# A hybrid decoder step on one core: GpSimd's weight split for the mixers in half-size instructions

## The chip, the cores and the metric
One Trainium2 chip, one of its cores. The metric is device time in microseconds (us) from the start to the end of one execution; lower is better. Five engines of the core work side by side, each through its own queue of instructions in order, and wait for each other on semaphores: TensorE (matmuls; PE in the profile, its weight loads PEld), VectorE (DVE), ScalarE (ACT), GpSimd (POOL) and SyncE (SP, which issues DMAs here).

## What is computed
Two layers of a hybrid decoder over 512 prompt tokens and 32 sample tokens (8 sequences of 4), all float32. Cut to what matters here:

```python
xn = _rmsnorm(h, g_mix)
proj = jnp.einsum('bld,de->ble', xn, w_in)             # inputs of three mixers
o_a = gla(...)        # gated linear attention, 4 heads, chunks of 64
o_m = mlstm(...)      # matrix memory, 4 heads
o_d = diff_attention(...)   # differential attention, paged cache for the samples
gates = jax.nn.sigmoid(jnp.einsum('bld,de->ble', xn, w_gate)).reshape(B, L, 3, D)
merged = (gates[:, :, 0] * jnp.einsum('blv,vd->bld', o_a, w_a)
          + gates[:, :, 1] * jnp.einsum('blv,vd->bld', o_m, w_m)
          + gates[:, :, 2] * jnp.einsum('blv,vd->bld', o_d, w_d))
h = h + jnp.einsum('bld,de->ble', merged, w_out)
h = h + (silu(rms(h) @ w_ffn_gate) * (rms(h) @ w_ffn_up)) @ w_ffn_down
h = h + sigmoid(rms(h) @ w_ple_gate) * (p_l @ w_ple_proj)
```

## The kernel before
Activations lie transposed: 128 channels on the partitions, 544 tokens (512 + 32) along a row. Each weight matrix is cut into chunks of up to 8 blocks of 128 x 128 (`raw`, 1024 columns, 512 KB). Each chunk is split in two for the matmuls: `wH`, the weight rounded to the matmul's format (fp32r), and `wL`, the rest (`raw` minus `wH`). TensorE multiplies wH by xH, wH by xL and wL by xH for each block, in two halves of 272 tokens, so that a chunk is 48 matmuls (line 536, `blocks_product`). Four buffers hold `raw`, two hold `wH` and two `wL`: the split of chunk n waits until TensorE has done chunk n - 2 (`chunk_done`), and TensorE's chunk n waits for `wl_split`. SyncE's load of chunk n waits for the `wl_split` of chunk n - 4.

Outside the mixers ScalarE makes `wH` (lines 465, 520 and 1851) and GpSimd `wL` (lines 469 and 528). In the mixers ScalarE has other work, and GpSimd makes both (`both_loop`, lines 481 and 484): 60 chunks a layer, named ml, df, merge0, merge1 and merge2, 12 each. Between its `wH` and its `wL` GpSimd waits for its own signal `wh_split`.

In that stretch TensorE's order is written out by hand: the small matmuls of the three mixers, and between them pieces of the next chunks' products, a quarter of a chunk each (`fill`). A piece that opens a new output waits for `out_taken`, which VectorE signals as it takes the output two before from PSUM (lines 688, 1744, 1754 and 1758, with the sequencer's signals at 1746 and 1755). VectorE does these takings in its own queue, behind its part of the mixers: the cumulated gates of gla (lines 954 to 965), the rotation of q and k (1212 to 1218), the keys and scores of the mLSTM (1239 to 1271), the softmax weights of the attention (`maxima` 1540; `weights` 1547 to 1550), the scaling and splitting of a branch's output (674 and 680; the latter signals `bn_l`, for which the last branch products wait), the sample's softmax (1580 to 1582) and the sum of the merged branches (1760). After the pieces between the attention's steps, what is left of merge2 is multiplied chunk by chunk without a break (`fill.rest`).

Of the kernel before, what the change touches and what calls it, by code (L numbers as in the profile page):

```python
# [28 lines left out]
F32 = mybir.dt.float32  # L29
F32R = mybir.dt.float32r  # L30
I32 = mybir.dt.int32
ALU = mybir.AluOpType
# [3 lines left out]
P = 128  # L36
D = 1024
KD = D // P
# [19 lines left out]
RAW, SPLIT = 4, 2  # L58
# [36 lines left out]
def program(nc, a, c, o):  # L95
    ctx = ExitStack()
    with ctx:
# [37 lines left out]
        ones = fixed.put("ones", [P, P])  # L135
# [35 lines left out]
        raw = [ws.put(f"raw{i}", [P, KMAX, P]) for i in range(RAW)]  # L171
        wH = [ws.put(f"wH{i}", [P, KMAX, P], F32R) for i in range(SPLIT)]
        wL = [ws.put(f"wL{i}", [P, KMAX, P], F32R) for i in range(SPLIT)]
# [122 lines left out]
        s, sems = Semaphores(), []  # L296
# [175 lines left out]
        def both_loop(pool, name, count=12, per=4):  # L472

            base = CHUNK[name]
            with pool.Fori(0, count // per) as i:
                for j in range(per):
                    n = base + j
                    pool.wait_ge(s.w_in[n % RAW], w_count(n, i, per))
                    pool.wait_ge(s.chunk_done, n + per * i - (SPLIT - 1))

                    pool.tensor_tensor(wH[n % SPLIT][:, :, :], raw[n % RAW][:, :, :],  # L481
                                       ones[:, 0:1].unsqueeze(1).to_broadcast([P, KD, P]), ALU.mult).then_inc(s.wh_split, 1)
                    pool.wait_ge(s.wh_split, n + 1 + per * i)
                    pool.tensor_tensor(wL[n % SPLIT][:, :, :], raw[n % RAW][:, :, :], wH[n % SPLIT][:, :, :].bitcast(F32),  # L484
                                       ALU.subtract).then_inc(s.wl_split, 1)

        def w_count(slot_chunk, i, per):

            slot = slot_chunk % RAW
            more = 48 if slot == CHUNK["small"] % RAW and slot_chunk >= CHUNK["small"] else 0  # L490
            return 16 * (slot_chunk // RAW + 1) + more + 16 * (per // RAW) * i
# [216 lines left out]
        with nc.Fori(0, DEPTH) as layer:  # L708
# [4 lines left out]
            with nc.Block() as block:  # L713
# [154 lines left out]
                @block.gpsimd  # L868
                def _(pool):
                    for n in range(SPLIT):  # L870
                        low_chunk(pool, n)
                    for k in range(1, KD):
                        add_square(pool, 0, k, sq0)
                    for n in range(SPLIT, 4):
                        low_chunk(pool, n)
                    low_loop(pool, "gla", 12, lambda j: KD, first=1)
                    low_loop(pool, "small", 1, lambda j: KD, per=1)
                    for name in ("ml", "df", "merge0", "merge1", "merge2"):
                        both_loop(pool, name)
                    low_loop(pool, "out", 8, lambda j: KD)  # L880
                    low_loop(pool, "ffn", 2 * KF, lambda j: KD)
                    low_loop(pool, "down", 4 * KD, lambda j: DOWN_K[j % 4][1], per=8)
                    for n in range(10):
                        low_chunk(pool, CHUNK["ple"] + n)
# [1342 lines left out]
```

## Time and profile before
| | |
|---|---|
| median of 3 runs | 2559.25 us (2553.18 to 2563.7) |
| the profiled execution | 2556.49 us |
| its span, first to last instruction | 2554.7 us |
| TensorE busy | 2359.1 us (92%) |
| VectorE busy | 1067.4 us (42%) |
| GpSimd busy | 1051.9 us (41%) |
| ScalarE busy | 690.3 us (27%) |

An engine's busy time is the union of its instructions; waits of its sequencer are not in it. The two layers run the same program (the mixers of layer 0 lie at about 116 to 755 us, those of layer 1 at 1370 to 2008). In the lists, "A <- B: us, times, longest" means that engine A stood idle until B released it. A row of the timeline gives the start, the duration, the engine, the line, the operation, what it writes and reads, and in brackets the idle time before it. A duration on VectorE or GpSimd counts from the instruction's start, also where it then waits for something inside it.

### The profile page before, as it was taken

To read this page: it belongs to the slowest core of one execution; us is meant where nothing else is said; L and a number is where in the kernel's file an instruction comes from. 1 tells how busy PE (TensorE), PEld (TensorE's weight loads), DVE (VectorE), ACT (ScalarE), POOL (GpSimd) and SP (SyncE) were. 2 spreads that over 40 slices of the span, in tenths; PEclk is the share of its full clock that TensorE was granted. 3 is DMA by queue.
4 is the path that set the end of the run, shared out by engine and by line. 5 is a ranking of instruction groups with operands and counts; after the bars stand their busy time and mean duration, and the time that the engine had idled before them with its cause. 6 is when DMAs were issued, how large, how long until landed. Compare 5 with 4: busy or idle time off the path is not lost. (4 is left out here: it accounts for less than half of the span.)

```text
span 2554.7 us, 43509 instructions
## 1 busy us (share of the span) xinstructions
PE 2359.1 (92%) x17974; PEld 2263.6 (89%) x17974; DVE 1067.4 (42%) x1289; ACT 690.3 (27%) x1006; POOL 1051.9 (41%) x472
## 2 busy tenths in 40 slices
PE   4989898989999999999969998978999999999996
PEld 3978797878899999999968988977898999999995
DVE  3173653641335443312534537356224444342236
ACT  3130313322214222222232131233222332222222
POOL 3444344432454444344344443434336444444431
PEclk9999899998999999999989999989899999999998
DMA  3522315223332332223135141331332323232221
GB/s 99 143 58 61 75 50 107 63 76 91 92 116 85 91 88 84 77 87 100 34 95 130 51 97 40 53 113 55 100 113 70 114 87 90 83 88 77 89 85 43
DMA packets 370870, 213.87 MB, mean 84 GB/s; under 512 B 34290, under 2 KB 356950, under 8 KB 370210
## 3 DMA queue, kind: packets, MB, share of 16 engines
q1 hardware_dynamic: 369186, 205.11, 29.3%
q10 hardware_dynamic: 1536, 6.69, 0.7%
q8 instruction: 106, 1.74, 0.3%
q14 instruction: 42, 0.34, 0.1%
HBM read 195.88 MB, written 15.88 MB: 83 GB/s over the span
## 5 line engine op out<-in xcount | busy, mean ns | idle before, releaser
L536 PE MATMUL G<-xH,wH 128*128 128x272 f32 x3616 | 789.6, 300 | 76.0 <-DVE xL L596 43.0
L536 PE MATMUL G<-xH,wL 128*128 128x272 f32 x3616 | 761.9, 293 | 0.0
L536 PE MATMUL G<-xL,wH 128*128 128x272 f32 x3616 | 760.9, 293 | 0.0
L536 PEld LDWEIGHTS G<-xH,wH 128*128 128x128 f32 x3616 | 581.2, 193 | 106.7 <-issue 54.2
L528 POOL TENSOR_TENSOR wL<-raw,wH 128x1024 fp32r<-128x1024 f32 (+2 forms) x186 | 421.3, 2265 | 599.1 <-ACT wH L1851 290.4
L536 PEld LDWEIGHTS G<-xL,wH 128*128 128x128 f32 x3616 | 583.3, 193 | 0.0
L536 PEld LDWEIGHTS G<-xH,wL 128*128 128x128 f32 x3616 | 579.4, 194 | 0.0
L481 POOL TENSOR_TENSOR wH<-raw,ones 128x1024 fp32r<-128x1024 f32 x120 | 234.3, 1953 | 698.0 <-PE G L536 691.9
L484 POOL TENSOR_TENSOR wL<-raw,wH 128x1024 fp32r<-128x1024 f32 x120 | 301.7, 2514 | 9.4
L465 ACT ACTIVATE wH<-raw 128x1024 fp32r<-128x1024 f32 (+2 forms) x116 | 105.5, 911 | 375.6 <-PE G L536 344.4
L1851 ACT ACTIVATE wH<-raw 128x1024 fp32r<-128x1024 f32 x82 | 87.0, 1061 | 325.8 <-PE G L536 325.8
L536 PE MATMUL G<-hidH,wL 128*128 128x272 f32 x704 | 145.7, 288 | 0.0
L536 PE MATMUL G<-hidH,wH 128*128 128x272 f32 x704 | 145.5, 288 | 0.0
L536 PE MATMUL G<-hidL,wH 128*128 128x272 f32 x704 | 145.1, 288 | 0.0
L469 POOL TENSOR_TENSOR wL<-raw,wH 128x1024 fp32r<-128x1024 f32 x28 | 71.0, 2539 | 153.1 <-ACT wH L465 153.1
L1809 DVE TENSOR_TENSOR h<-G,h 128x544 f32<-128x544 f32 x32 | 23.2, 725 | 253.3 <-PE G L536 235.5
L1890 DVE TENSOR_TENSOR f_u<-G,rB 128x544 f32<-128x544 f32 x44 | 31.9, 725 | 224.2 <-PE G L536 224.2
L1900 DVE TENSOR_TENSOR hidL<-f_u,hidH 128x544 f32 (+1 forms) x44 | 123.0, 2796 | 0.4 <-DVE hidL L1900 0.4
L536 PEld LDWEIGHTS G<-hidH,wH 128*128 128x128 f32 x704 | 110.7, 188 | 0.0
L536 PEld LDWEIGHTS G<-hidL,wH 128*128 128x128 f32 x704 | 110.6, 189 | 0.0
L536 PEld LDWEIGHTS G<-hidH,wL 128*128 128x128 f32 x704 | 109.9, 189 | 0.0
L1744 DVE TENSOR_TENSOR u_g<-G,rB 128x544 f32<-128x544 f32 x48 | 34.6, 721 | 141.0 <-PE G L536 140.1
(345 smaller groups left out, 3043.3 us busy)
## 6 DMA issues: line engine op xcount, KB each, us to landing
raw<-in_w_in SPq DMA_DIRECT2D x72, 512.0 KB, 3.8
raw<-in_w_gate SPq DMA_DIRECT2D x48, 512.0 KB, 3.8
raw<-in_w_ffn_gate SPq DMA_DIRECT2D x44, 512.0 KB, 3.8
raw<-in_w_ffn_up SPq DMA_DIRECT2D x44, 512.0 KB, 3.8
raw<-in_w_branch SPq DMA_DIRECT2D x24, 512.0 KB, 3.5
raw<-in_w_ffn_down SPq DMA_DIRECT2D x32, 384.0 KB, 3.3
raw<-in_w_ffn_down SPq DMA_DIRECT2D x32, 320.0 KB, 3.1
d_kr<-in_cache_k SPq DMA_DIRECT2D x32, 256.0 KB, 2.9
```

The costliest lines, as they stand in the source:

```text
L465: act.activation(wH[n % SPLIT][:, 0:kb, :], raw[n % RAW][:, 0:kb, :], ACT.Copy).then_inc(s.wh_split, 1)
L469: pool.tensor_tensor(wL[n % SPLIT][:, 0:kb, :], raw[n % RAW][:, 0:kb, :], wH[n % SPLIT][:, 0:kb, :].bitcast(F32), ALU.subtract).then_inc(s ...
L481: pool.tensor_tensor(wH[n % SPLIT][:, :, :], raw[n % RAW][:, :, :], ones[:, 0:1].unsqueeze(1).to_broadcast([P, KD, P]), ALU.mult).then_inc ...
L484: pool.tensor_tensor(wL[n % SPLIT][:, :, :], raw[n % RAW][:, :, :], wH[n % SPLIT][:, :, :].bitcast(F32), ALU.subtract).then_inc(s.wl_split, 1)
L528: pool.tensor_tensor(wL[n % SPLIT][:, 0:kb(j), :], raw[n % RAW][:, 0:kb(j), :], wH[n % SPLIT][:, 0:kb(j), :].bitcast(F32), ALU.subtract).t ...
L536: mm = pe.matmul(G[:, slot, half, 0:HALF], w[n % SPLIT][:, wk, :], x[:, xk, half * HALF:(half + 1) * HALF], start=(start and at == 0 and w ...
L1744: dve.tensor_tensor(halves(u), out2(out % 2), halves(rB[:, :]), ALU.mult).then_inc(s.u_lin, 1)
L1809: dve.tensor_tensor(halves(h[:, m, :]), out2((OUT[name] + m) % 2), halves(h[:, m, :]), ALU.add).then_inc(sem, 1)
L1851: act.activation(wH[n % SPLIT][:, :, :], raw[n % RAW][:, :, :], ACT.Copy).then_inc(s.wh_split, 1)
L1890: dve.tensor_tensor(halves(f_u[:, u, :]), out2((out + 1) % 2), halves(rB[:, :]), ALU.mult).then_inc(s.out_taken, 1)
L1900: dve.tensor_tensor(lo.rearrange("p o n -> p (o n)"), f_u[:, u, :], hi.rearrange("p o n -> p (o n)").bitcast(F32), ALU.subtract).then_inc( ...
```

## The change
In `both_loop`, each of the two GpSimd instructions of a chunk (8 row blocks, 1024 columns) is issued as two of four row blocks (512 columns), one behind the other with no wait between them. The first of a pair signals nothing; the second signals what the one instruction signalled. The wait on `wh_split` stays between the pair for `wH` and the pair for `wL`. The data, the buffers and all else are the same.

```diff
-                    pool.tensor_tensor(wH[n % SPLIT][:, :, :], raw[n % RAW][:, :, :],
-                                       ones[:, 0:1].unsqueeze(1).to_broadcast([P, KD, P]), ALU.mult).then_inc(s.wh_split, 1)
+                    for k in (0, KD // 2):
+                        half = slice(k, k + KD // 2)
+                        turned = pool.tensor_tensor(wH[n % SPLIT][:, half, :], raw[n % RAW][:, half, :],
+                                                    ones[:, 0:1].unsqueeze(1).to_broadcast([P, KD // 2, P]), ALU.mult)
+                    turned.then_inc(s.wh_split, 1)
                     pool.wait_ge(s.wh_split, n + 1 + per * i)
-                    pool.tensor_tensor(wL[n % SPLIT][:, :, :], raw[n % RAW][:, :, :], wH[n % SPLIT][:, :, :].bitcast(F32),
-                                       ALU.subtract).then_inc(s.wl_split, 1)
+                    for k in (0, KD // 2):
+                        half = slice(k, k + KD // 2)
+                        turned = pool.tensor_tensor(wL[n % SPLIT][:, half, :], raw[n % RAW][:, half, :],
+                                                    wH[n % SPLIT][:, half, :].bitcast(F32), ALU.subtract)
+                    turned.then_inc(s.wl_split, 1)
```

## Rows read from the trace of the kernel before

**Rows 1.** The page, part 1: busy time, share of the span, instructions.
```profile
PE 2359.1 (92%) x17974; PEld 2263.6 (89%) x17974; DVE 1067.4 (42%) x1289; ACT 690.3 (27%) x1006; POOL 1051.9 (41%) x472
```

**Rows 2.** Windows, layer 0's mixers: engines' busy time, clock, DMA share, GB/s.
```profile
116.00:755.00 639.00, 585.59 (x4370) 544.27 (x4369) 295.23 (x427) 161.38 (x275) 275.81 (x123) 0.93 0.29 76
```

**Rows 3.** Waits of PE, 116 to 755 us: total, times, longest.
```profile
PE G L536 <- DVEq L1755: 10.1, 4, 3.5
PE G L536 <- DVE B L688: 7.8, 1, 7.8
PE G L536 <- DVEq L1746: 6.1, 4, 3.1
PE G L536 <- issue: 5.3, 1, 5.3
...
PE M L1356 <- DVEq L1239: 4.4, 1, 4.4
PE M L1389 <- DVE m_SD L1271: 2.9, 1, 2.9
```

**Rows 4.** Waits, whole span: GpSimd's first line.
```profile
POOL wH L481 <- PE G L536: 691.9, 117, 15.2
```

**Rows 5.** Timeline of POOL and of PEld in merge2's unbroken chunks.
```profile
735.13 2.76 POOL L484 TENSOR_TENSOR wL<-raw,wH 128x1024 fp32r<-128x1024 f32 x1
...
738.74 0.19 PEld L536 LDWEIGHTS G<-xH,wH 128*128 128x128 f32 x1
```

**Rows 6.** Timeline of POOL, DVE and PE, 517 to 530 us (attention).
```profile
517.30 1.89 POOL L481 TENSOR_TENSOR wH<-raw,ones 128x1024 fp32r<-128x1024 f32 x1 [5.31 <-PE G L536]
519.28 2.40 POOL L484 TENSOR_TENSOR wL<-raw,wH 128x1024 fp32r<-128x1024 f32 x1
...
517.38 2.10 DVE L1549 TENSOR_SCALAR d_w<-d_e,d_rc 128x512 f32<-128x512 f32 x1
519.52 2.71 DVE L1550 SCALAR_TENSOR_TENSOR d_w<-d_e,d_rc,d_w 128x512 f32<-128x512 f32 x1
522.15 0.71 DVE L1754 TENSOR_TENSOR MG<-G,u_g 128x544 f32<-128x544 f32 x1
...
523.06 0.65 PE L536 MATMUL G<-xH,wH 128*128 128x272 f32 x2 [3.50 <-DVEq L1755]
...
528.77 0.49 DVE L1549 TENSOR_SCALAR d_w<-d_e,d_rc 128x512 f32<-128x512 f32 x1
529.30 0.75 DVE L1550 SCALAR_TENSOR_TENSOR d_w<-d_e,d_rc,d_w 128x512 f32<-128x512 f32 x1
```

**Rows 7.** Timeline of POOL and DVE, 273 to 285 us (rotation and branch scaling).
```profile
273.64 1.89 POOL L481 TENSOR_TENSOR wH<-raw,ones 128x1024 fp32r<-128x1024 f32 x1 [2.79 <-PE G L536]
275.61 2.73 POOL L484 TENSOR_TENSOR wL<-raw,wH 128x1024 fp32r<-128x1024 f32 x1
...
274.06 2.05 DVE L1216 SCALAR_TENSOR_TENSOR d_t<-d_t,d_sin 128x544 f32<-128x544 f32 x1 [0.15 <-DVE C L1213]
276.14 2.78 DVE L1218 TENSOR_TENSOR C<-C,d_t 128x544 f32<-128x544 f32 x1
279.15 2.62 DVE L674 SCALAR_TENSOR_TENSOR oraw_g<-oraw_g,ghead,rO_g 128x1088 f32<-128x1088 f32 x2 [0.23 <-DVE C L1218]
...
283.37 0.73 DVE L1216 SCALAR_TENSOR_TENSOR d_t<-d_t,d_sin 128x544 f32<-128x544 f32 x1 [0.15 <-DVE C L1213]
```

**Rows 8.** Line 484: duration ns min/median/max, first and last start, forms.
```profile
L484 POOL TENSOR_TENSOR wL<-raw,wH x120: 2342/2388/3286, 123.8 to 1990.4; 128x1024 fp32r<-128x1024 f32 x120
```

**Rows 9.** Groups by line and form: busy us, mean ns, idle us before.
```profile
L528 POOL TENSOR_TENSOR wL<-raw,wH 128x640 fp32r<-128x640 f32 x32 | 50.2, 1568 | 80.8 <-ACT wH L465 80.8
...
L1218 DVE TENSOR_TENSOR C<-C,d_t 128x544 f32<-128x544 f32 x16 | 36.3, 2267 | 0.5
```

**Rows 10.** Timeline of POOL, first instructions of the program.
```profile
0.25 0.10 POOL L2212 MEMSET const-float32-0.0<- 128x1 f32 x1 [0.25 <-issue]
0.29 0.10 POOL L2212 MEMSET const-float32-1.0<- 128x1 f32 x1
```

## The prediction

> **What bounds the kernel now.** I read the page's first part [rows 1]: TensorE is busy for 92% of the span, GpSimd for 41%. So TensorE sets the time, and another engine matters only where TensorE stands still for it. The window over the mixers of layer 0 shows where it does: from 116 to 755 us TensorE is busy for 585.59 of 639 us, at a mean granted clock of 0.93 [rows 2]. The list of waits [rows 3] names who ended the idle time there. VectorE's instructions, or its sequencer after one of them (DVEq), stand behind nearly all of it; GpSimd is not on the list. The 5.3 us put down to "issue" are VectorE's too: there TensorE waits for bn_l, which VectorE's L680 signals. The second layer repeats the pattern, so all sums are made for one layer and doubled.
>
> GpSimd's own idle time stands in the list of its waits [rows 4]: 117 times, 691.9 us, it waited for TensorE to finish the chunk before, ahead of L481. It has room. But how much at the tightest place? At 733 to 739 us TensorE does chunk after chunk with nothing between. The wL there ends at 735.13 + 2.76 = 737.89, and TensorE's first weight load of that chunk starts at 738.74 [rows 5]: cover 0.85 us. Of the 60 chunks of a layer the eight between 697 and 745 us, worked out in this way, have 0.85 to 1.29; nearly all others have more.
>
> **How GpSimd and VectorE meet.** Look at the form columns and durations of VectorE in [rows 6]. L1549 at 528.77 takes 0.49 and L1550 0.75 us while GpSimd is idle. At 517.38 and 519.52 the same two take 2.10 and 2.71. GpSimd's wH runs from 517.30 to 519.19 and its wL from 519.28 to 521.68: each VectorE instruction ends 0.3 to 0.6 us after the GpSimd instruction under which it began. So a VectorE instruction that reads SBUF twice (or TENSOR_SCALAR from SBUF) waits out a whole GpSimd instruction; those that read PSUM (L1754, 0.71) don't. And a waiting VectorE instruction gets in between wH and wL although only 0.08 us lie there: [rows 7] has L1216, ending at 276.11, 0.58 us after wH's end at 275.53 (0.73 when free, so 0.15 was already done), and that wL takes 2.73 where the least is 2.34 [rows 8]; the entry cost GpSimd 0.39, VectorE's 0.73 less some 0.35. These are the constants of the sum.
>
> **The change, part by part.** The pieces, signals and waits of every other engine stay. Removed: 2 instructions of 1024 columns a chunk (120 chunks). Added: 4 of 512. No DMA, no wait and no semaphore count changes. The first of a pair signals nothing, the second signals for both.
>
> Cost of a half. The trace has no 512-column instruction on GpSimd. wL has 640 columns at 1.57 us [rows 9] and 1024 at 2.34 us at least [rows 8]: 2.0 ns a column and 0.28 fixed. A half of wL is then 0.28 + 512 x 0.00202 = 1.31 us; with the same fixed part a half of wH is 0.28 + 1.61 / 2 = 1.09. What four halves take beyond the two wholes of a chunk is A. Upper end by the fit: 2 x (0.28 + 0.08 between instructions) = 0.71 us a chunk. Upper end without the fit: each half as dear as 640 columns, 4 x 1.57 - 1.89 - 2.34 = 2.05. Lower end: two GpSimd instructions without a wait between them start 0.04 us apart though each takes 0.10 [rows 10], so A = 0.07 if the fixed parts overlap; a gain is excluded, since the columns are the same. I take A = 0.4, midway between the fit and the overlap, the nearest rows. The cover of 0.85 hides it at the tightest chunks, so on TensorE's path through GpSimd it costs nothing; if A passed 0.85, each of those eight chunks would pay the rest.
>
> What it gives: VectorE's waits get shorter, if it can also get in between two halves. Chain at 517 [rows 6], worked out: first half of wH ends at 517.30 + 1.09 = 518.39; L1549 ends 0.35 later, 518.74; L1550 arrives and waits for the second half, 518.39 + 1.09 + 0.14 (L1549's entry) = 519.62, and ends 0.61 later, 520.23, not 522.23. L1754 and then TensorE at 523.06 move up by 2.0 of the 3.50 us idle.
>
> Chain at 274 [rows 7] shows the limit: L1216 and L1218 gain in the same way, about 2.1 us, but the two L674 behind them, free before (2.62 us for both), now meet the two halves of wL. GpSimd's work is the same in all; only a chain whose lock-taking instructions run out early gets past it. By the same constants L674 ends at 281.5, not 281.77: 0.25 saved of the 4.4.
>
> The other chains in the same way, from the starts of their VectorE and GpSimd rows, saved per layer, against the waits in [rows 3]: the gates before B L688 (7.8): 1.9. Four before L1755 (10.1): 2.0, 0.8, 0.75 and 0. Four before L1746 (6.1): 1.2, 0.75, 0.6 and 0.44, the last two being all that was idle. Before m_SD (2.9): 1.1. L680 (5.3): 2.0. Before L1239 (4.4): 0.25. Ahead of L1702 one VectorE instruction (L1581) arrives past the middle of wL and would meet its dearer second half: minus 0.3. Sum 11.5 us a layer, 23 in both. What is late next is in each case TensorE's own queue, since these waits are shorter than what was idle, or end it.
>
> The Trainium skill says of this port (SBUF — State Buffer, Who interferes with whom) that it is an exclusive lock for the whole instruction; by that rule, the trace agrees with 2.10 against 0.49 us, each half is a lock of its own and the forecast stands. The Trainium skill says also (GPSIMD Engine Reference, 2.1 Instruction dispatch) that a GpSimd core starts the next instruction as soon as it is done with its share, while others still work; by that the port may never come free between two unsignalled halves, and the result would be the first rival's.
>
> **The sum.** The profiled execution took 2556.5 us (span 2554.7 and 1.8 around it), 0.1% under the median of the runs, 2559.25. 2556.5 - 23 = 2533.5; against the median 2536.
>
> **Rivals.**
> No entry between halves: wH and wL carry a wait between them, the two halves of one don't, and the only unsignalled neighbours in the trace overlap [rows 10]. Then VectorE waits as long as before plus A / 2 for a wait on one pair and A for both. About 0.3 us for each of 11 chains with idle behind them is 3.3 a layer, 6.6 in both: 2566 (2560 at A = 0.07). For it: those overlapping starts. Against: a waiting VectorE instruction won every 0.08 us gap.
> The pair itself is dear: no entry, and A over 0.8. The waits of the 11 chains grow by three quarters of A, 22 x 0.6 = 13 us at A = 0.8, which is the point of 0.5%, and from 0.85 the eight tightest chunks of each layer pay too: at A = 1.1, 22 x 0.83 = 18 and some 3 for these, 2580. For it: no row shows 512 columns and wH's fixed part is unknown. Against: 512 columns lie only 128 beyond the 640 of [rows 9].
> Gain beyond the sum: the granted clock falls to its lower level, 1.2 GHz, behind several of the idle stretches, and the mean of 0.93 over 639 us [rows 2] means some 90 us at that level a layer (0.07 x 639 / 0.5). If shortened stretches spare a third of it, that is 15 us of work more in each layer: 2510 with some of it lost. Which stretch brings the clock down these rows don't tell, so I don't count on it.
>
> **How the numbers follow.** Forecast 0.48, with a range of its own from 2522 to 2548. No entry 0.31. Dear pair 0.15. Beyond the sum 0.06. Some 0.5% (12.8 us, 2546.5 and 2572) is what a measurement of this kernel can tell from no change. Faster: nine tenths of the forecast less its weaker end, and all beyond: 0.46. Slower: nearly all of the dear pair and the tail of no entry: 0.17. Same: 0.37. The range runs from 2520 to 2576: it leaves out about half of the dear pair and most of the gain beyond, and little else.
>
> **What would show it.** L481 and L484 with 240 records each; start to start within a pair 1.1 and 1.3 us. Mean of L1218, 2.27 us now [rows 9], at 1.6 if VectorE gets in between halves, and above 2.3 if not; then records of the second half of wL, stretched by VectorE's entries, tell the same. TensorE's waits behind L1746 and L1755, 16 us a layer now, at 9 to 10. GpSimd's wL must still end before TensorE's first load at the merge2 chunks. The prediction is wrong if the halves run as one for the port, if a pair costs over 0.8 us more, or if TensorE, resumed earlier, only waits longer for ScalarE or VectorE at the next step.

## The result, and the profile after

The changed kernel takes 2496.3 us (median of 4 runs, 2493.9 to 2504.8) beside 2557.8 us for the kernel before on the same chip: ratio 0.976 (0.974 to 0.979), a gain of 61 us where 23 were forecast. It was measured a second time among the experiments: 2506.2 beside 2555.0, ratio 0.982 (0.979 to 0.984), a gain of 49. The profiled execution took 2504.8 us, the longest of its four, 51.7 us less than the profiled one of before. The comparison of the traces is about those 51.7.

In the changed file all lines behind the first pair are six further down: L536 is now L542, L1218 L1224, L1550 L1556, L1744 L1750, L1754 L1760; `wH` is made at L483 and `wL` at L489.

Part 1 of the page (after), to be held against [rows 1]:
```profile
PE 2337.0 (93%) x17974; PEld 2243.3 (90%) x17974; DVE 1015.1 (41%) x1289; ACT 690.6 (28%) x1006; POOL 1114.2 (45%) x712
```
GpSimd has 240 instructions more and works 62 us longer, VectorE 52 us less with the same number of instructions: the time that it stood waiting inside them. TensorE does the same 17974 matmuls in 22 us less. Its idle time (span less busy) goes from 195.6 to 166.0.

The mixers of both layers as windows (from the same instruction to the same instruction), before and then after; the columns are those of [rows 2]: PE, PEld, DVE, ACT, POOL busy, clock:
```profile
116.00:755.70 639.70, 585.59 (x4370) 544.29 (x4370) 295.93 (x428) 162.08 (x276) 275.81 (x123) 0.93 0.29 76
1369.90:2005.00 635.10, 584.85 (x4373) 543.73 (x4371) 295.26 (x428) 162.12 (x276) 275.21 (x123) 0.94 0.29 77
```
```profile
116.00:723.60 607.60, 568.31 (x4370) 527.83 (x4370) 269.08 (x428) 162.11 (x276) 306.62 (x243) 0.96 0.30 80
1338.30:1952.90 614.60, 575.16 (x4373) 534.77 (x4371) 269.44 (x428) 162.37 (x276) 306.62 (x243) 0.95 0.30 79
```
32.1 and 20.5 us are gone here, slightly more than the span lost. Of these 52.6 us, 25.6 were idle time of TensorE (54.1 and 50.2 before, 39.3 and 39.4 now) and 27.0 were its own working time, for the same matmuls at a higher mean clock. That split is the main reading of the case: two gains of about the same size, of which the forecast counted one. The two layers aren't alike: layer 0 lost 14.8 us of idle time, layer 1 10.8. The difference lies mainly in TensorE's wait for VectorE's B (L688, now L694), which went from 7.8 to 5.4 us in layer 0 but from 4.2 to 5.4 in layer 1.

The waits of PE, layer 0's mixers, after, beside [rows 3]:
```profile
PE G L542 <- DVE B L694: 5.4, 1, 5.4
PE M L1626 <- ACT d_e L1483: 5.2, 1, 5.2
PE G L542 <- DVEq L1761: 4.6, 3, 2.4
PE M L1362 <- DVEq L1245: 3.8, 1, 3.8
PE G L542 <- DVEq L1752: 3.5, 3, 2.3
PE G L542 <- issue: 3.3, 1, 3.3
...
PE M L1395 <- DVE m_SD L1277: 1.3, 1, 1.3
```
Every wait named in [rows 3] is shorter in this layer, and no new one of weight has taken its place.

The two lines of GpSimd (after): durations of one in ns as least/median/most; beside [rows 8]:
```profile
L483 POOL TENSOR_TENSOR wH<-raw,ones x240: 1033/1040/2872, 121.8 to 1937.3; 128x512 fp32r<-128x512 f32 x120
```
```profile
L489 POOL TENSOR_TENSOR wL<-raw,wH x240: 1259/1286/3482, 124.0 to 1939.7; 128x512 fp32r<-128x512 f32 x120
```
Undisturbed halves start 1.00 us (wH) and 1.25 us (wL) apart, so each starts 0.04 us before the one ahead of it has ended.

The attention chain that [rows 6] shows, after the change; POOL, DVE, PE:
```profile
502.97 2.49 POOL L483 TENSOR_TENSOR wH<-raw,ones 128x512 fp32r<-128x512 f32 x2 [3.82 <-PE G L542]
505.53 2.54 POOL L489 TENSOR_TENSOR wL<-raw,wH 128x512 fp32r<-128x512 f32 x2
...
502.51 0.49 DVE L1555 TENSOR_SCALAR d_w<-d_e,d_rc 128x512 f32<-128x512 f32 x1
503.03 1.52 DVE L1556 SCALAR_TENSOR_TENSOR d_w<-d_e,d_rc,d_w 128x512 f32<-128x512 f32 x1
504.48 0.71 DVE L1760 TENSOR_TENSOR MG<-G,u_g 128x544 f32<-128x544 f32 x1
...
505.39 0.49 PE L542 MATMUL G<-xH,wH 128*128 128x272 f32 x2 [0.61 <-DVEq L1761]
```
L1556 meets the first half of wH, which would end at about 504.0, and ends at 504.55, while GpSimd still has the second half of the same tile to do. It got in between two halves with no wait between them. Before, the same instruction lasted until wL was through, 2.71 us. TensorE's idle time at this place falls from 3.50 to 0.61 us.

### The profile page after: what moved, and what is told of

The parts are those of the page before. It is cut to its first block and busy times, and to the rows that moved or that the text cites. A ratio compares the mean times of both kernels' runs of the same rounds, so it can differ in the third digit from the quotient of the medians.

```text
span 2503.0 us, 43749 instructions
## 1 busy us (share of the span) xinstructions
PE 2337.0 (93%) x17974; PEld 2243.3 (90%) x17974; DVE 1015.1 (41%) x1289; ACT 690.6 (28%) x1006; POOL 1114.2 (45%) x712
## 5 line engine op out<-in xcount | busy, mean ns | idle before, releaser
L542 PE MATMUL G<-xH,wH 128*128 128x272 f32 x3616 | 786.0, 299 | 61.4 <-DVE xL L602 40.3
L542 PE MATMUL G<-xH,wL 128*128 128x272 f32 x3616 | 759.3, 292 | 0.0
L542 PE MATMUL G<-xL,wH 128*128 128x272 f32 x3616 | 757.6, 291 | 0.0
L534 POOL TENSOR_TENSOR wL<-raw,wH 128x1024 fp32r<-128x1024 f32 (+2 forms) x186 | 421.5, 2266 | 599.8 <-ACT wH L1857 290.4
L542 PEld LDWEIGHTS G<-xH,wH 128*128 128x128 f32 x3616 | 577.5, 192 | 92.5 <-issue 41.5
L542 PEld LDWEIGHTS G<-xL,wH 128*128 128x128 f32 x3616 | 579.9, 192 | 0.0
L542 PEld LDWEIGHTS G<-xH,wL 128*128 128x128 f32 x3616 | 576.6, 193 | 0.0
L483 POOL TENSOR_TENSOR wH<-raw,ones 128x512 fp32r<-128x512 f32 x240 | 267.1, 1133 | 583.8 <-PE G L542 578.7
L489 POOL TENSOR_TENSOR wL<-raw,wH 128x512 fp32r<-128x512 f32 x240 | 331.3, 1401 | 9.4
L542 PE MATMUL G<-hidH,wL 128*128 128x272 f32 x704 | 145.8, 289 | 0.0
L542 PE MATMUL G<-hidH,wH 128*128 128x272 f32 x704 | 145.6, 288 | 0.0
L542 PE MATMUL G<-hidL,wH 128*128 128x272 f32 x704 | 145.1, 288 | 0.0
L469 POOL TENSOR_TENSOR wL<-raw,wH 128x1024 fp32r<-128x1024 f32 x28 | 70.9, 2536 | 151.9 <-ACT wH L465 151.9
L542 PEld LDWEIGHTS G<-hidH,wH 128*128 128x128 f32 x704 | 110.7, 188 | 0.0
L542 PEld LDWEIGHTS G<-hidL,wH 128*128 128x128 f32 x704 | 110.7, 189 | 0.0
L542 PEld LDWEIGHTS G<-hidH,wL 128*128 128x128 f32 x704 | 109.9, 189 | 0.0
L1750 DVE TENSOR_TENSOR u_g<-G,rB 128x544 f32<-128x544 f32 x48 | 34.5, 719 | 162.5 <-PE G L542 162.0
```

The costliest lines, as they stand in the source:

```text
L469: pool.tensor_tensor(wL[n % SPLIT][:, 0:kb, :], raw[n % RAW][:, 0:kb, :], wH[n % SPLIT][:, 0:kb, :].bitcast(F32), ALU.subtract).then_inc(s ...
L483: turned = pool.tensor_tensor(wH[n % SPLIT][:, half, :], raw[n % RAW][:, half, :], ones[:, 0:1].unsqueeze(1).to_broadcast([P, KD // 2, P]) ...
L489: turned = pool.tensor_tensor(wL[n % SPLIT][:, half, :], raw[n % RAW][:, half, :], wH[n % SPLIT][:, half, :].bitcast(F32), ALU.subtract)
L534: pool.tensor_tensor(wL[n % SPLIT][:, 0:kb(j), :], raw[n % RAW][:, 0:kb(j), :], wH[n % SPLIT][:, 0:kb(j), :].bitcast(F32), ALU.subtract).t ...
L542: mm = pe.matmul(G[:, slot, half, 0:HALF], w[n % SPLIT][:, wk, :], x[:, xk, half * HALF:(half + 1) * HALF], start=(start and at == 0 and w ...
L1750: dve.tensor_tensor(halves(u), out2(out % 2), halves(rB[:, :]), ALU.mult).then_inc(s.u_lin, 1)
```

## The experiments

All are variants of these lines. Ratios are against the kernel before. "Idle" is span less TensorE's busy time; "mixers" gives the length of the two layers' mixers, as in the windows above; "at the lower level" is the time, from the clock's records, at which 1.2 GHz was granted instead of 2.4 in each of them, worked out from the traces as a whole; "long" is how many stretches of 20 us or more at the lower level lie in the sample attention, and in which layer. All columns behind the ratio belong to the one profiled execution. For wL alone and for halves everywhere that was the fastest of its four, 11 and 16 us under the median.

| kernel | median us | ratio (95%) | idle | PE busy | mixers | at the lower level there | long |
|---|---|---|---|---|---|---|---|
| before | 2555.0 to 2559.3 | 1 | 195.6 | 2359.1 | 639.7, 635.1 | 86, 79 | 2 |
| after | 2496.3 | 0.976 (0.974 to 0.979) | 166.0 | 2337.0 | 607.6, 614.6 | 45, 59 | 1, layer 1 |
| the same again | 2506.2 | 0.982 (0.979 to 0.984) | 169.5 | 2329.8 | 613.0, 606.1 | 56, 45 | 1, layer 0 |
| wH alone | 2508.8 | 0.982 (0.980 to 0.985) | 172.7 | 2328.1 | 611.1, 611.1 | 41, 41 | 0 |
| wL alone | 2531.5 | 0.991 (0.989 to 0.994) | 190.1 | 2328.9 | 620.1, 618.6 | 52, 46 | 0 |
| quarters | 2487.3 | 0.974 (0.971 to 0.976) | 159.5 | 2322.4 | 601.1, 600.8 | 35, 35 | 0 |
| 7 + 1 blocks | 2512.3 | 0.982 (0.979 to 0.985) | 180.1 | 2331.2 | 621.2, 613.0 | 62, 45 | 1, layer 0 |
| 1 + 7 blocks | 2522.6 | 0.986 (0.983 to 0.989) | 173.5 | 2349.7 | 621.6, 620.3 | 66, 63 | 2 |
| split left out | 2464.1 | 0.964 (0.962 to 0.966) | 139.9 | 2325.0 | 588.1, 595.4 | 31, 49 | 1, layer 1 |
| maxima twice | 2502.2 | 0.979 (0.978 to 0.981) | 174.9 | 2325.4 | 609.1, 610.8 | 38, 41 | 0 |
| maxima four times | 2543.6 | 0.996 (0.994 to 0.998) | 196.2 | 2344.5 | 624.9, 635.0 | 48, 66 | 1, layer 1 |
| late at four places | 2526.3 | 0.989 (0.987 to 0.990) | 187.0 | 2334.3 | 621.2, 620.2 | 51, 50 | 0 |
| halves everywhere | 2506.7 | 0.983 (0.979 to 0.986) | 170.6 | 2318.5 | 605.0, 603.0 | 44, 35 | 0 |
| quarters and halves | 2484.9 | 0.973 (0.971 to 0.974) | 162.9 | 2320.4 | 601.4, 599.1 | 44, 31 | 0 |

**One pair alone.** wH in halves, wL whole:
```diff
-                    for k in (0, KD // 2):
-                        half = slice(k, k + KD // 2)
+                    for k, e in ((0, KD),):                      # the wL loop
+                        half = slice(k, e)
```


> Only wH is made in two halves; wL is one instruction again. Port theory (VectorE waits for the end of the GpSimd instruction under which it began, and gets in between halves): a chain of three VectorE instructions now meets both halves of wH and then the whole of wL (2.05 us) where before the third ran free, so such chains lose about 0.4 us, and only the short ones (gates before L688, m_kw, L680, the pair at 517) gain 0.8 to 1 each. 5 to 25 us under the kernel before, well under half of the change's 61. Rival A (each shortened wait is worth its own length, whatever follows): 27 us, since 0.9 of 1.95 us of lock time a chunk goes with wH. Rival B (the gain is not the port but the number or spacing of GpSimd's instructions): half of it, 30.


and the other way round, wL in halves and wH whole:

> Only wL is made in two halves; wH is one instruction again. Port theory: the first VectorE instruction of a chain waits for all of wH as before, the second and third for a half of wL each, 2 x 1.1 against one wait of 2.05; chains of two gain 1.0. 10 to 30 us under the kernel before, and with the other single pair less than the 61 of both. Mean of L1218 (it begins 0.54 us into wL) falls to 1.6 to 1.7 us as in the changed kernel. Rival A: 34 us. Rival B: 30 us.


Measured: 50 us less by wH alone and 27 by wL alone (medians, beside 2558.5 us for before), 77 in sum beside the 49 to 61 of the whole change. In idle time the two don't overlap: 22.9 us less by wH alone and 5.5 by wL alone, 28.4 in sum, beside 29.6 and 26.1 for the whole change. It is TensorE's working time that doesn't add up: 31.0 and 30.2 us less in the two, 22.1 and 29.3 with both. So the gain of wL alone is nearly all clock. The profile of the first shows where its expectation went wrong. It added up how long each VectorE instruction waits, and L1224 indeed waits nearly as long as before:
```profile
L1224 DVE TENSOR_TENSOR C<-C,d_t 128x544 f32<-128x544 f32 x16 | 33.6, 2099 | 0.5
```
But TensorE waits for the end of a chain. The chain of [rows 6] with wH alone in halves (POOL, DVE, PE):
```profile
505.90 2.22 POOL L483 TENSOR_TENSOR wH<-raw,ones 128x512 fp32r<-128x512 f32 x2 [4.84 <-PE G L542]
508.19 2.70 POOL L489 TENSOR_TENSOR wL<-raw,wH 128x1024 fp32r<-128x1024 f32 x1
...
505.98 1.24 DVE L1555 TENSOR_SCALAR d_w<-d_e,d_rc 128x512 f32<-128x512 f32 x1
507.25 1.41 DVE L1556 SCALAR_TENSOR_TENSOR d_w<-d_e,d_rc,d_w 128x512 f32<-128x512 f32 x1
508.59 0.71 DVE L1760 TENSOR_TENSOR MG<-G,u_g 128x544 f32<-128x544 f32 x1
...
509.50 0.49 PE L542 MATMUL G<-xH,wH 128*128 128x272 f32 x2 [1.34 <-DVEq L1761]
```
GpSimd and VectorE meet just as in [rows 6]: L1555 starts 0.08 us after wH in both. There L1550 began 0.24 us after wL (519.52 and 519.28), and had to wait it out whole (2.71). Here L1555 gets in between the halves, L1556 behind the second one, and both are done before wL's work begins: the whole wL is harmless, and TensorE's idle time here falls from 3.50 us to 1.34. This is the chain that the prediction worked out for the full change: it had the two VectorE instructions end 1.44 and 2.93 us after wH's start, and here they end after 1.32 and 2.76. What counts in this chain is how many entries lie ahead of its last port instruction.

**7 + 1 blocks: longest hold against number of entries.** The longest hold stays seven eighths of before's, the number of entries is that of the change.
```diff
-                    for k in (0, KD // 2):
-                        half = slice(k, k + KD // 2)
+                    for k, e in ((0, 7), (7, KD)):               # both loops
+                        half = slice(k, e)
```


> Both pairs are made as two instructions, as in the change, but of seven and one row blocks (896 and 128 columns): the same number of instructions, signals and waits, and about the same GpSimd time; the longest hold of the port is 1.7 and 2.1 us, not 1.0 and 1.3. Port theory: 0 to 12 us under the kernel before, perhaps slower, since a VectorE instruction that follows the first is caught by the short one as well. Rival B (number or spacing of the instructions): all of the 61 us.


It gained 46 us, nearly as much as wH in halves (50), against 0 to 12 expected of the hold's length. Part of that is clock: its idle time is 15.5 us less than before, with wH in halves 22.9. The chain of [rows 6] in that kernel, all engines:
```profile
508.40 2.22 POOL L483 TENSOR_TENSOR wH<-raw,ones 128x896 fp32r<-128x896 f32 x2 [4.11 <-PE G L542]
508.48 1.89 DVE L1555 TENSOR_SCALAR d_w<-d_e,d_rc 128x512 f32<-128x512 f32 x1
...
510.40 0.77 DVE L1556 SCALAR_TENSOR_TENSOR d_w<-d_e,d_rc,d_w 128x512 f32<-128x512 f32 x1
510.70 2.42 POOL L489 TENSOR_TENSOR wL<-raw,wH 128x896 fp32r<-128x896 f32 x1
511.10 0.71 DVE L1760 TENSOR_TENSOR MG<-G,u_g 128x544 f32<-128x544 f32 x1
...
512.01 0.49 PE L542 MATMUL G<-xH,wH 128*128 128x272 f32 x2 [1.35 <-DVEq L1761]
```
L1555 waits out the seven blocks of wH (1.89 us, 2.10 before). L1556 then waits only for the one block that follows and is done before wL's long part starts: 0.77 instead of 2.71 us. The long part has no one left to hold up in this chain.

The order turned round, one block first:
```diff
+                    for k, e in ((0, 1), (1, KD)):               # both loops
```


> As the run of seven and one row blocks, but the short one first (128 and 896 columns). Entry theory (a VectorE instruction costs at most one GpSimd instruction, whichever it meets, so a chain ends earlier the more entries it is offered ahead of the long ones): four instructions a chunk, four entries, so again most of the gain; the first instruction of a chain arrives 0.1 to 0.6 us into wH and meets the long one mostly, the second the short one of wL: 2500 to 2530. Longest-hold theory (refuted by seven and one, unless its order matters): near the kernel before, 2545 to 2560.


2522.6, in the range expected. L1224's mean is the lowest of the kernels that make both wH and wL in two parts (0.83 us), the total is the worst of them, and two long stretches at the lower clock level lie in its profile. Idle time alone (173.5) puts it beside wH in halves (172.7): the rest of its distance is clock. Halves, 7 + 1 and 1 + 7 offer the same number of entries and save 26 to 30, 15.5 and 22 us of idle time. So the number of entries isn't all: how long the parts are, and in which order, counts too.

**Quarters.** Four instructions of two blocks for each tile:
```diff
+                    for k, e in ((0, 2), (2, 4), (4, 6), (6, KD)):   # both loops
```


> Both are made in quarters (256 columns). The halves cost 0.28 us more a chunk (wH's start to wL's end 4.64 against 4.36); quarters then 0.84. Port theory: each wait is 0.55 to 0.65 at most, chains of three gain another 0.9 us over halves; some 10 to 25 us under the changed kernel, unless the last unbroken chunks of merge2, with 0.45 us of cover left under halves, run out of it: 0.85 - 0.84 leaves none at three chunks a layer, under 3 us in all. Rival B (number or spacing): more than with halves as well, so this run tells sizes, not causes. If what is left of TensorE's idle time isn't the port's: no gain, 0 to 5 us slower than the changed kernel.


2487.3 us, a gain of 71. Mean of L1224, then TensorE's waits for GpSimd (both from the kernel with quarters):
```profile
L1224 DVE TENSOR_TENSOR C<-C,d_t 128x544 f32<-128x544 f32 x16 | 16.0, 999 | 0.6
```
```profile
PE G L542 <- POOL wL L489: 4.0, 3, 3.0
```
```profile
697.38 2.82 POOL L489 TENSOR_TENSOR wL<-raw,wH 128x256 fp32r<-128x256 f32 x4
...
700.25 0.30 PEld L542 LDWEIGHTS G<-xH,wH 128*128 128x128 f32 x2
```
Here the extra GpSimd time shows for the first time. At merge2's unbroken chunks wL ends at 700.20 and the load starts at 700.25: the cover is down to 0.05 us. The longest wait of all, 3.0 us near 148, was for VectorE's B before (7.8) and is for GpSimd now. GpSimd's 97 us more than in the changed kernel buy 6.5 us less idle.

**The split left out: how much the port costs in all.** GpSimd works one column of each tile, its signals and waits stay:
```diff
-                        half = slice(k, k + KD // 2)
+                        half = slice(k, k + 1)        # and [:, half, 0:1] of each tile, once instead of twice
```


> In the mixers GpSimd works on one column only of each chunk's wH and wL (1 of 1024, one instruction each): most of the weight split is left out there, so the mixers multiply stale weights. The signals, the loads and all other instructions stay. It shows the whole of what GpSimd's instructions cost there. Port theory: VectorE's instructions take their free times (L1549, L1550 and L1218 at 0.3 to 0.75 us), and the time is below quarters: what 35 us of VectorE's waits a layer in the changed kernel still cost, 2465 to 2485. TensorE's idle time that ScalarE (L1620, 5.2), TensorE's own order or DMA causes stays. If the gain of the change came from the number or spacing of GpSimd's instructions and not from its holding the port: near the kernel before, 2540 or more, since there are fewer instructions than ever.


```profile
L1224 DVE TENSOR_TENSOR C<-C,d_t 128x544 f32<-128x544 f32 x16 | 11.6, 725 | 0.5
```
2464.1 us. So GpSimd's work on the split costs the kernel before some 91 us, of which 55.7 are idle time of TensorE and 34.1 its working time; halves take back 49 to 61 of them, quarters 71. That it is the port rests on L1224, which takes its free 0.73 us here, and on the waits of [rows 3], none of which is for GpSimd. The matmuls of this kernel multiply stale weights, so its results are wrong, and no run shows whether other values alone change the clock. This is a floor for this way of cutting, not a kernel that one could use.

**More VectorE time that needs no port.** The attention's maxima, which read PSUM, taken twice, then four times:
```diff
+                        for _ in range(3):                           # once for "twice"
+                            step(dve.tensor_reduce(d_nm[:, 0:2], M[:, 0:2, 0:width], AX.X, ALU.max, negate=True))
                         dve.tensor_reduce(d_nm[:, 0:2], M[:, 0:2, 0:width], AX.X, ALU.max, negate=True).then_inc(s.nm_ready, 1)
```


> The changed kernel, with the row maximum of each attention step taken twice (L1546, reads PSUM, doesn't wait for GpSimd's port): 0.42, 0.69, 0.96 and 1.23 us, four times each, some 14 us a layer more on VectorE with the port left alone. It asks what a late VectorE costs TensorE. If TensorE's clock falls because it stands idle: idle time comes back at the takings of L1750 and L1760, time at the lower clock with it, and the span grows by more than the idle time does (before against after: 52 us of span, 30 us of idle). 15 to 40 us over the changed kernel. If clock and idle time have nothing to do with each other: the span grows by the idle time alone. If TensorE's queue hides it: 0 to 5 us.


Some 14 us of VectorE work more in each layer moved the median by 6 us or less: VectorE as such is not what binds the mixers.

> The changed kernel, with the row maximum of each attention step taken four times: some 42 us a layer more on VectorE, none of it at GpSimd's port. Twice (14 us a layer) brought 4 us of TensorE's idle time a layer and 6 us in all, too little to judge the clock by. Here the takings of L1750 and L1760 must come 2 us late at most of the 16 steps; idle time of 15 to 30 us a layer more. If the lower clock follows TensorE's idle time: time at 1.2 GHz grows from 150 to 175 us in all towards the 229 of the kernel before or over it, TensorE's busy time grows with it (2337 in the changed kernel's profile, 2359 before), and the span grows by more than the idle time. If the clock went up in the changed kernel for a reason of its own (what GpSimd and VectorE do at their port, say): busy time stays at 2325 to 2337, and the span grows by the idle time alone.


With some 40 us more a layer (the added instructions are busy for 79.1 us in all) it is. The page's part 1 of that kernel:
```profile
PE 2344.5 (92%) x17974; PEld 2243.8 (88%) x17974; DVE 1087.5 (43%) x1385; ACT 688.2 (27%) x1006; POOL 1110.5 (44%) x712
```
The idle time is that of the kernel before (196.2 and 195.6), the matmuls are the same, and yet TensorE works 14.6 us less. Idle time in total doesn't settle the clock.

**Long idle stretches.** Perhaps it is the length of single stretches. Four delays in each layer's attention, each stretch 3 to 4 us:
```diff
+                        for _ in range({3: 10, 7: 6, 11: 5, 15: 4}.get(n, 0)):
+                            step(dve.tensor_reduce(d_nm[:, 0:2], M[:, 0:2, 0:width], AX.X, ALU.max, negate=True))
```


> The changed kernel, with VectorE held up at four of the sixteen attention steps only: the row maximum of steps 3, 7, 11 and 15 is taken 11, 7, 6 and 5 times, 4.2 to 4.9 us more at each, 18 us a layer, again without GpSimd's port. Four times at every step brought 28 us of idle time in all, in stretches of 1 to 3.4 us, and 11 us of TensorE's busy time; the kernel before has the same idle time in all, with stretches of 3 to 8 us, and 26 us more of busy time than the changed one. Here most of the added idle time should lie in stretches of 2.5 to 4 us, some 20 to 25 us in both layers. If the length of the stretches decides how much is lost at the lower clock: busy time 15 us or more over the changed kernel's 2330 to 2337, in spite of the smaller idle time, and 2535 to 2545. If it doesn't: busy time up by 5 to 10, 2525 to 2533.


```profile
PE M L1667 <- ACT d_wT L1491: 11.5, 3, 4.3
```
The waits are there, three of the four seen in this line, up to 4.3 us, and near each one a stretch at the lower level began (3.4 to 6.8 us long). Still TensorE's busy time is 2334.3, within the 2329.8 to 2337.0 of the changed kernel and 25 under that of before. Of the two cases named ahead, the one in which they bring back 15 us or more fell.

**The changed kernel again**, to see how far its clock differs from one profile to the next:

> The changed kernel once more, on the chip and beside the runs of these two, as their reference: 2494 to 2505, clock 0.965 to 0.970 against 0.952 to 0.958 of the kernel before.


The two profiles of one kernel differ by 3.7 us of span and 7.2 us of busy time, and the long stretch at the lower level lies in layer 1 in one and in layer 0 in the other.

**Can more be had?** Halves for the other two places where GpSimd makes wL (L469, L534), with halves and with quarters in the mixers:
```diff
-            pool.tensor_tensor(wL[n % SPLIT][:, 0:kb, :], raw[n % RAW][:, 0:kb, :], wH[n % SPLIT][:, 0:kb, :].bitcast(F32),
-                               ALU.subtract).then_inc(s.wl_split, 1)
+            for k, e in ((0, kb // 2), (kb // 2, kb)):
+                turned = pool.tensor_tensor(wL[n % SPLIT][:, k:e, :], raw[n % RAW][:, k:e, :],
+                                            wH[n % SPLIT][:, k:e, :].bitcast(F32), ALU.subtract)
+            turned.then_inc(s.wl_split, 1)
```


> The changed kernel, with GpSimd's wL outside the mixers in halves as well (L469 and L528). There TensorE runs chunk after chunk, idle for 20 to 21 us in all behind xL (L602) and at each layer's start, where VectorE's xL and the squares wait for the port. Port theory: VectorE's hidL (2.9 us), h (2.8) and xL get shorter by about a us each, but behind only the xL ones TensorE waits: 0 to 6 us under the changed kernel. If cover runs out in the chunks made by ScalarE and GpSimd together: a few us over it.

> Quarters in the mixers and halves elsewhere, the two put together: what quarters gave (about 9 us under the changed kernel) plus what halves elsewhere give, 2480 to 2490. If the second set pays nothing, the same as quarters alone, 2487.


2506.7 (2490.9 to 2514.9), nothing certain beside the changed kernel; and 2484.9 (2484.2 to 2485.2), the fastest of the kernels that make the whole split, though its interval overlaps that of quarters alone. The places outside the mixers give little or nothing; quarters in the mixers are what beats the changed kernel, by 10 to 20 us.

## The clock: what of it is explained

The second half of the gain is TensorE's working time. In the windows of the mixers it is 585.6 and 584.9 us before, and 568 to 575 after. The table separates two things.

The first is plain. Leave the long stretches of 20 us out, and what is left at the lower level goes with the idle time of the same mixers: 31 and 29 us at 25 idle (split left out), 35 and 35 at 35 (quarters), 35 to 45 at 38 to 40 (after, in both profiles), 46 to 52 at 49 to 50 (wL alone, late at four places), 65 and 58 at 54 and 50 (before). From the first to the next to last that is 20 us for 25 of idle: 0.8 us at half clock, or some 0.4 us of working time, for each microsecond of idle. A straight line through the mixers of all profiles but before's is flatter, 0.65 us. The 25.6 us of idle saved then bring some 8 to 10 us along.

The clock's records also say behind which idle stretches these shorter ones come. In layer 0 of the kernel before, ten of the eleven begin during an idle stretch of 1.98 us or more or within 1.5 us of its end. The one behind L1389 (2.94 us idle for m_SD) lasts 6.8 us; the changed kernel waits 1.31 us there, and its clock stays up. Windows of these 6.8 us, before and then after:
```profile
304.80:311.60 6.80, 6.80 (x29) 6.13 (x28) 1.76 (x7) 1.14 (x4) 0.38 (x1) 0.50 0.00 0
```
```profile
299.70:306.50 6.80, 6.79 (x56) 6.26 (x57) 3.59 (x10) 1.14 (x4) 1.95 (x2) 1.00 0.01 2
```
In the same way the 3.4 us behind the idle stretches at 523 and 549 are gone (3.50 and 1.98 us idle before, 0.61 and 0.57 now), and behind those at 153 and 459 (7.84 and 3.21 before, 5.38 and 2.37 now) 3.4 us less each lie at the lower level. These five sum to 20.4 us; in all, the shorter stretches of layer 0 shrank by 20.2 us.

The second are the long stretches. They lie in the sample attention, with its matmuls of four columns, which does the eight sequences in two passes of four in each layer; a long stretch begins within a pass. The kernel before has one in each layer, in the first pass both times. The window from L1702 to L1722 in the first pass of layer 0 in the kernel before, and the same matmuls in the changed one:
```profile
583.70:609.60 25.90, 25.86 (x137) 25.55 (x137) 2.94 (x6) 0.95 (x2) 4.25 (x2) 0.60 0.22 61
```
```profile
561.80:579.80 18.00, 17.94 (x137) 17.64 (x137) 2.94 (x6) 0.71 (x2) 4.53 (x4) 0.91 0.32 88
```
137 matmuls in both, TensorE without a gap, a granted clock of 0.60 and of 0.91, and 7.9 us between them. Single rows show the two levels, first before, then after:
```profile
596.19 3.41 PE L1718 MATMUL M<-d_wTs,d_V 128*128 128x4 f32 x16
```
```profile
575.43 1.84 PE L1724 MATMUL M<-d_wTs,d_V 128*128 128x4 f32 x16
```
What went ahead is nearly alike: 1.11 us idle before the first of these matmuls in the kernel before, 1.39 in the other. In the changed kernel the long stretch is in the second pass of layer 1. That pass in its layer 0 and in its layer 1:
```profile
610.20:623.60 13.40, 13.40 (x115) 13.32 (x115) 1.51 (x2) 0.04 (x1) 4.96 (x5) 1.00 0.27 80
1830.90:1853.70 22.80, 22.80 (x115) 22.75 (x115) 1.51 (x2) 0.06 (x1) 4.93 (x5) 0.55 0.16 47
```
The two mixers of one kernel differ by 7.0 us (after) and 6.9 us (again), in both the ones with the long stretch being longer. Over the profiles there are none in seven, one in five and two in two, one of these the kernel before. So a part of the 52 us is one long stretch fewer, some 8 or 9 us (7.9 and 9.4 between the windows above), and by the other profiles it could have been none or two.

That makes 16 to 19 of 27. The other 8 to 11 are before's, whose shorter stretches sum to 58 to 65 us where kernels with as much idle time have 45 to 52. I have no test that settles why; the same idle stretch of 3.21 us at L536 is followed by 6.8 us at the lower level in layer 0 and by 3.4 in layer 1. Neither the idle time in total (maxima four times) nor four longer stretches of it (late at four places) bring it back. It isn't one unlucky profile: in 34 executions of the kernel before the mean clock was 0.952 to 0.958, in 8 of the changed one 0.961 to 0.970. What triggers the long stretches, and why before is slowed more than its idle time accounts for, stays open.

## Why the prediction was wrong, by its steps

**GpSimd's extra time: right.** Halves of 1.04 and 1.29 us were forecast as 1.09 and 1.31. Start to start they were 1.00 and 1.25. From wH's start to wL's end a chunk in merge2 takes 4.64 us instead of 4.36, so A = 0.28, where 0.4 was taken. It is hidden, as said (after, merge2's unbroken chunks; compare [rows 5]):
```profile
703.67 2.53 POOL L489 TENSOR_TENSOR wL<-raw,wH 128x512 fp32r<-128x512 f32 x2
...
706.65 0.31 PEld L542 LDWEIGHTS G<-xH,wH 128*128 128x128 f32 x2
```
wL ends at 706.20, cover 0.45 us, and TensorE doesn't wait in these chunks.

**VectorE enters between halves: right**, and "no entry" and "the pair itself is dear" fell. The mean of L1224 is 1.41 us (2.27 before [rows 9]; 1.6 forecast, over 2.3 without entry). The two rules that the prediction weighed come out so. That the port is held for the whole instruction (the Trainium skill, SBUF — State Buffer, Who interferes with whom) fits each half being a hold of its own. That GpSimd's cores start the next instruction before all are done (the Trainium skill, GPSIMD Engine Reference, 2.1 Instruction dispatch) fits the overlap of 0.04 us, but the overlap doesn't keep a waiting VectorE out.

**The idle time: right in mechanism, somewhat small.** By wait, a layer, forecast and then measured in layer 0: before B 1.9, 2.4; the four of L1755 3.55, 5.5; the four of L1746 3.0, 2.6; m_SD 1.1, 1.6; L680 2.0, 2.0; L1239 0.25, 0.6; L1702 minus 0.3, minus 0.3. Sum 11.5, and 14.4. The waits behind L1746 and L1755 sum to 8.1 (forecast 9 to 10). The one term that is off is L1755, above all at 523 us: 2.0 forecast, 2.9 measured. The starts of [rows 6] were kept as they stand, but upstream savings shift GpSimd against VectorE. There, wH now starts 0.46 us after L1555 instead of 0.08 before it, so that one port instruction slips through ahead of it. In all the mixers lost 25.6 us of idle, with 23 forecast, in the repeated profile about the same (TensorE's idle over the span 26 less). That the total is so near is in part luck: the sum of one layer was doubled, but layer 0 lost 14.8 us and layer 1 10.8, since the wait for B grew by 1.2 us there where 1.9 less were forecast.

**The clock: the step that failed.** The prediction had the right window, 0.93 in [rows 2], and wrote out that it stood for some 90 us a layer at the lower level, that sparing a third would be 15 us a layer, and gave it 0.06, because the rows "don't tell" which stretch brings the clock down, "so I don't count on it". The term was left out of the sum, though nothing supported zero, and the trace in hand did tell: windows behind the idle stretches show a granted clock of 0.50 (304.80 to 311.60 above). So it was to be expected that fewer and shorter idle stretches would leave less time at the lower level. Measured: 41 and 20 us less at the lower level (86 to 45, 79 to 59), 27 us of working time, of which 8 to 11 stay open as said above. With half of the rival's 30 in the sum the forecast would have been 2521, with all of it 2506; the range, which ended at 2520, left out a case for which the working stood on the page.

## What to carry to other kernels

Where GpSimd works beside VectorE chains on which TensorE waits, cut its long instructions into parts without a wait between them as long as GpSimd has cover for the extra 0.14 us or so of each added part (0.28 us for two more instructions a chunk): what counts most is how many places a chain's port instructions find to enter, and equal parts saved more idle time here than 7 + 1 or 1 + 7. Work out such a change from the last instruction of each chain, never from the sum of the single waits. And when a change shortens TensorE's idle stretches, put the working time that comes back with the clock into the sum and not only among the rivals: here it was as large as the idle time itself, though about a third of it isn't explained.

## What the runs showed of the hardware beyond what was expected

- One block in eight, cut off at the end of each tile, gives a gain of 46 us beside 49 to 61 for halves: in the chain shown, the hold of 2.42 us delays none of the three VectorE instructions, since those that need the port got in ahead of it.
- GpSimd's time by columns, without disturbance: wL 0.71 us for 256, 1.26 for 512, 1.57 for 640 [rows 9] and 2.34 for 1024 [rows 8]; a quarter of wH 0.61, a half 1.03.
- The same 137 matmuls took 25.9 us in one profile and 18.0 in another at granted clocks of 0.60 and 0.91, with no gap in either, and one kernel does both in its two layers: 22.8 and 13.4 us for the same 115 matmuls.
